# Scan stage of a gated linear recurrence: 32-row key-value products, output in token order

## The reference, cut to what matters

```
def gla_chunk_scan(q, k, v, g, s0):              # L = 32
    b = jnp.cumsum(g, axis=2)
    scores = einsum('nblhk,nbmhk->nbhlm', q * exp(b - b_mid), k * exp(b_mid - b))
    o_intra = einsum('nbhlm,nbmhv->nblhv', where(tri, scores, 0.0), v)
    q_dec, k_dec, decay = q * exp(b), k * exp(b[:, :, -1:] - b), exp(b[:, :, -1])
    def step(s, xs):
        qd, kd, vv, dc = xs
        o = einsum('blhk,bhkv->blhv', qd, s)
        s = dc[..., None] * s + einsum('blhk,blhv->bhkv', kd, vv)
        return s, o
...
    def readout(o, zg):
        on = rms_norm(o, norm_g)                 # over the 128 features of a head
        return (on * silu(zg)) @ w_out
```

## Time and profile before

| | us |
|---|---|
| median of 3 runs | 4289.17 (4285.29 to 4294.36) |
| the profiled execution | 4288.58 |
| its span in the profile | 4286.9 |
| TensorE busy in the span | 4009.6 (94%) |
| VectorE busy | 3233.5 (75%) |
| ScalarE busy | 1963.4 (46%) |

### The profile page before, as it was taken

One profiled execution on the slowest core, in us unless ns is written; L12 is line 12 of the kernel. 1 busy time (PEld: TensorE's weight loads), 2 busy tenths in 40 slices (PEclk: granted clock), 3 DMA queues, 4 the chain that ended last, 5 costly groups with the idle time before them and its releaser, 6 DMA issues. The chain is left out here.

```text
span 4286.9 us, 62093 instructions
## 1 busy us (share of the span) xinstructions
PE 4009.6 (94%) x20354; PEld 3426.2 (80%) x20354; DVE 3233.5 (75%) x5926; ACT 1963.4 (46%) x3726; POOL 1163.7 (27%) x906
## 2 busy tenths in 40 slices
PE   8997988999999899999989999878899999899998
PEld 2886877788888688888867777657899999899997
DVE  2689789998987588888874645558987777577777
ACT  2212235777777522222234434333477778433333
POOL 0322213434333344444422111123122222122221
PEclk9998999999999999999999999889999999999999
DMA  7443126999999899999941111012588888899996
GB/s 285 158 138 128 49 69 228 311 327 350 321 343 338 308 391 373 377 376 374 372 179 50 40 39 39 20 69 69 193 280 273 274 281 296 297 333 331 332 336 225
DMA packets 411882, 1026.06 MB, mean 239 GB/s; under 512 B 33968, under 2 KB 182448, under 8 KB 405680
## 3 DMA queue, kind: packets, MB, share of 16 engines
q1 hardware_dynamic: 296496, 604.22, 39.9%
q0 software_dynamic: 110592, 402.70, 26.2%
q10 hardware_dynamic: 4608, 16.78, 1.1%
HBM read 904.03 MB, written 119.54 MB: 239 GB/s over the span
## 5 line engine op out<-in xcount | busy, mean ns | idle before, releaser
L136 ACT ACTIVATE w_hi<-w_raw 128x1024 fp32r<-128x1024 f32 x536 | 568.3, 1061 | 1152.2 <-PE psum L1425 878.8
L168 PE MATMUL psum<-h_hi,w_hi 128*128 128x512 f32 (+1 forms) x2208 | 877.9, 398 | 90.9 <-PEq L809 30.9
L170 PE MATMUL psum<-h_hi,w_lo 128*128 128x512 f32 (+1 forms) x2208 | 840.8, 381 | 0.0
L169 PE MATMUL psum<-h_lo,w_hi 128*128 128x512 f32 (+1 forms) x2208 | 840.5, 381 | 0.0
L147 DVE TENSOR_TENSOR w_lo<-w_raw,w_hi 128x1024 fp32r<-128x1024 f32 x424 | 519.5, 1225 | 423.5 <-ACT w_hi L136 400.8
L1423 PE MATMUL psum<-a_hie,w_hi 128*128 128x512 f32 (+1 forms) x2048 | 759.1, 371 | 31.0 <-DVE a_loe L1496 31.0
L1425 PE MATMUL psum<-a_hie,w_lo 128*128 128x512 f32 (+1 forms) x2048 | 756.4, 369 | 0.0
L1424 PE MATMUL psum<-a_loe,w_hi 128*128 128x512 f32 (+1 forms) x2048 | 752.1, 367 | 0.0
L1295 POOL DMA_INDIRECT u_rowsg<-in_peer_u_rows,expert_idx x384 | 443.6, 1155 | 1102.8 <-DVE u_rowsg L1052 978.6
L1404 POOL DMA_INDIRECT v_rowse<-in_peer_v,expert_idx x384 | 423.7, 1103 | 825.6 <-DVE row_sume L1505 812.6
L1227 ACT ACTIVATE ojg<-eq_jg,gate_Tg 128x128 fp32r<-128x128 bf16 x1792 | 547.0, 388 | 171.5 <-DVE eq_jg L1075 170.7
(11 more groups left out here) (266 smaller groups left out, 5725.5 us busy)
## 6 DMA issues: line engine op xcount, KB each, us to landing
w_raw<-in_peer_u SPq DMA_DIRECT2D x256, 512.0 KB, 5.9
w_raw<-in_peer_v SPq DMA_DIRECT2D x256, 512.0 KB, 5.7
gates<-stageg SPq DMA_DIRECT2D x28, 2048.0 KB, 16.1
acts<-act_gg SPq DMA_DIRECT2D x128, 256.0 KB, 5.0
gte<-gates SPq DMA_DIRECT2D x32, 1024.0 KB, 8.4
act_fe<-acts SPq DMA_DIRECT2D x128, 256.0 KB, 6.2
ada_w<-in_ada_w SPq DMA_DIRECT2D x12, 2048.0 KB, 8.1
ada_rows<-in_ada_w SPq DMA_DIRECT2D x48, 512.0 KB, 3.9
```

The costliest lines, as they stand in the source:

```text
L136: act.activation(self.weights(s)[0], self.raw[:, slot, :], ACT.Copy).then_inc(self.hi_done, 1)
L168: pe.matmul(out, wh, hi[:, k], start=(k == 0), stop=False)
L169: pe.matmul(out, wh, lo[:, k], start=False, stop=False)
L170: last = pe.matmul(out, wl, hi[:, k], start=False, stop=(k == KC - 1))
```

## The change: what it does, and the diff

Key-value products. A group is now eight matmuls instead of two: for each direction and each chunk r of the block, the 32 rows of that chunk of `kd_tok` and of `v_tok` itself, 128 columns wide, into bank r. `v_by_chunk`, its memset and its four copies per head are gone. All four banks are used by every group, so `kv_free` no longer lets TensorE run one group ahead.

Output. The result now lies in token order, in two halves of 256 tokens in two banks. The masked scores are the stationary side and `v_tok` the moving one; for the states, the 32 columns of `qd` are stationary and the 128-wide state is moving. ScalarE squares each block of 128 x 128 from PSUM and sums along the row in the same instruction; root and reciprocal are 128 x 2. VectorE multiplies from PSUM, TensorE turns the four blocks back (`turn_back`, L1727 in the changed kernel), and VectorE applies gain and gate half by half. The matmul with `ones` and the copy of the output are gone.

Order. On VectorE the next head's decays stand behind the first group and the two scans behind the third and the fourth, and the two query multiplications stand between the two masks. On TensorE the first keys are transposed without product steps ahead of them, two steps now stand behind the second scores, and three steps of tile 4 (two before) stand behind the output.

```
-                            last = pe.matmul(bank(2 * d + x % 2), kd_tok[d][:, g],
-                                             v_by_chunk[:, g].rearrange("p r x -> p (r x)"),
-                                             start=True, stop=True)
+                            for r in range(ROWS):
+                                rows = slice(r * CHUNK, (r + 1) * CHUNK)
+                                last = pe.matmul(bank(r)[:, d * P:(d + 1) * P], kd_tok[d][rows, g], v_tok[rows, g],
+                                                 start=True, stop=True)
...
-                    for d in range(2):
-                        for c in range(XCH):
-                            sl = slice(c * CHUNK, (c + 1) * CHUNK)
-                            last = pe.matmul(bank(3)[:, sl], state[d][:, c], qd[d][:, sl], start=False,
-                                             stop=(d == 1 and c == XCH - 1), skip_group_check=True)
...
+                    for half in range(2):
+                        out = blocks_of(bank(2 + half)[:, 0:2 * P])
+                        for d in range(2):
+                            for g in range(2):
+                                sl = slice((2 * half + g) * P, (2 * half + g + 1) * P)
+                                pe.matmul(out[:, g], probs[d][:, sl], v_tok[:, 2 * half + g],
+                                          start=(d == 0 and g == 0), stop=False, skip_group_check=True)
+                        for d in range(2):
+                            for x in range(2 * ROWS):
+                                c, r = 2 * ROWS * half + x, x % ROWS
+                                last = pe.matmul(out[r * CHUNK:(r + 1) * CHUNK, x // ROWS],
+                                                 qd[d][:, c * CHUNK:(c + 1) * CHUNK], state[d][:, c], start=False,
+                                                 stop=(d == 1 and x == 2 * ROWS - 1), skip_group_check=True)
+                        last.then_inc(S["o_mm"], 1)
...
                     for d in range(2):
-                        if more:
-                            tile(q, u + 1, 2, range(2 * d, 2 * d + 2))
+                        if more and d:
+                            tile(q, u + 1, 2, range(2))
                         to_tokens(h, d + 1)
                         scores(h, d)
+                    if more:
+                        tile(q, u + 1, 2, range(2, 4))
...
-                for x in ("tok_cp", "prob_done", "o_cp"):
+                for x in ("tok_cp", "prob_done", "y_done", "kv_free"):
                     pe.sem_inc(S[x], 1)
-                pe.sem_inc(S["kv_free"], 2)
...
-                            kv = t.psum[:, 4 + 2 * d + x % 2, r * P:(r + 1) * P]
+                            kv = t.psum[:, 4 + r, d * P:(d + 1) * P]
...
                         dve.sem_inc(S["kv_free"], 1)
+                        if more and x == 0:
+                            dve.wait_ge(S["tok_mm"], h * 3 + 3)
+                            decays(h + 1)
+                        elif more and x in (2, 3):
+                            scan(h + 1, x - 2)
```

More of the change, by code:

```diff
@@ L1640, in _ @@
                     m += 1
-                pool.memset(v_by_chunk[:], 0.0).then_inc(S["vc_zero"], 1)
                 def lo(q, j):
@@ L1741, in turn @@
                     if more:
-                        tile(*at, 4, range(KC // 2, KC - 2))
+                        tile(*at, 4, range(KC // 2, KC - 3))
                     output(h)
                     if more:
-                        tile(*at, 4, range(KC - 2, KC))
-                    pe.wait_ge(S["osq"], h + 1)
-                    pe.matmul(bank(2), t.ones[:], osq, start=True, stop=True).then_inc(S["osum"], 1)
-                for x in ("tok_cp", "prob_done", "o_cp"):
+                        tile(*at, 4, range(KC - 3, KC))
+                    turn_back(h)
+                for x in ("tok_cp", "prob_done", "y_done", "kv_free"):
                     pe.sem_inc(S[x], 1)
-                pe.sem_inc(S["kv_free"], 2)
                 for k in range(KC):
@@ L1862, in turn @@
                                           ALU.subtract).then_inc(S["d1"], 1)
-                    dve.wait_ge(S["tok_cp"], h * 3 + 2)
-                    def by_chunk(r0, r1):
-                        for r in range(r0, r1):
-                            rows = slice(r * CHUNK, (r + 1) * CHUNK)
-                            last = dve.tensor_copy(v_by_chunk[rows, :, r], v_tok[rows])
-                        return last
-                    by_chunk(0, ROWS // 2)
                     for d in range(2):
@@ L1888, in turn @@
                                                 S["prob_done"], 1)
+                    masked(0)
                     for d in range(2):
@@ L1891, in turn @@
                         dve.tensor_tensor(qd[d][:], qd[d][:], qs[:], ALU.mult).then_inc(S["qd_done"], 1)
+                    masked(1)
                     dve.wait_ge(S["dc_done"], h * 2 + 2)
-                    if more:
-                        dve.wait_ge(S["tok_mm"], h * 3 + 3)
-                        decays(h + 1)
                     at = 0
@@ L1924, in turn @@
-                    dve.wait_ge(S["y_done"], h + 1)
+                        if more and x == 0:
[3 more added lines that the diff above has]
+                            scan(h + 1, x - 2)
+                    out = [blocks_of(t.psum[:, 6 + half, 0:2 * P]) for half in range(2)]
+                    for half in range(2):
+                        two = slice(2 * half, 2 * half + 2)
+                        dve.wait_ge(S["oroot"], h * 2 + half + 1)
+                        dve.reciprocal(orn[:, two], orn[:, two]).then_inc(S["orstd"], 1)
+                        dve.wait_ge(S["orstd"], h * 2 + half + 1)
+                        dve.tensor_tensor(o[:, two], out[half], orn[:, two].unsqueeze(2).to_broadcast([P, 2, P]),
+                                          ALU.mult).then_inc(S["o_norm"], 1)
@@ new lines, in turn @@
+                    dve.wait_ge(S["z_in"], h + 1)
+                    for half in range(2):
+                        sl = slice(2 * half * P, 2 * (half + 1) * P)
+                        dve.wait_ge(S["o_turned"], h * 2 + half + 1)
+                        dve.scalar_tensor_tensor(out=y[:, bass.ds(h, 1), sl].rearrange("p a n -> p (a n)"),
+                                                 in0=t.psum[:, 4 + half, 0:2 * P], scalar=hs(t.gains[:, 5], h),
+                                                 in1=zs[:, u, sl], op0=ALU.mult, op1=ALU.mult).then_inc(S["y_done"], 1)
@@ L1925, in _ @@
+                    dve.wait_ge(S["y_done"], h * 2 + 3)
                 norm.vector(dve)
                 dve.wait_ge(S["reset_done"], 4)
-                dve.wait_ge(S["vc_zero"], 1)
                 decays(0)
+                for d in range(2):
+                    scan(0, d)
                 turns(dve, turn)
```

67 lines of the change are left out of this document (31 added, 36 removed).

## The result

The changed kernel takes 4194.06 us (median of 4, 4192.4 to 4203.76) against 4291.76 for the kernel before in the same series. The ratio is 0.978, 95% interval 0.977 to 0.980: 2.2% faster. The forecast was 4255 with a range of 4200 to 4285, so the sign was right and the size was not: 34 us were forecast from the profiled execution and about 97 came, which lies outside the range. Span in the profile: 4190.7 us, before 4286.9.

The account below looks back on a forecast made before the run. TensorE's own work, busy 94% of the span, was taken as the bound. The output's 4.8 us a head, seven times, gave 33.6 with the other terms at 0: 4288.6 - 33.6 = 4255 us, range 4200 to 4285.

Parts of the forecast that it names:

- What bounds the kernel, and the clock: TensorE's own work, busy 94% of the span, sets the time; a 128-wide moving side keeps the output at full clock.
- The output, 32 x 0.164: Output products with the states: 0.164 us each, between bounds 0.055 and 0.218; output 7.05 us, a gain of 4.8 per head.
- The key-value products, "I take 0.218": Each 32-row product costs 0.218 us, weight loading the floor; eight per group take 1.74 us as before, so no change.
- The chain of groups, value 0: TensorE and VectorE hand over at each group; TensorE idles about 2.5 us instead of 1.2, covered by what it won.
- the second rival: Key-value and output products both overlap: 4212 us at 0.109 each, 4185 at 0.055; chance 0.30.
- Keys, mask and end of the head, value 0: New 1.0 us key wait offsets the 1.01 us mask wait; the head's end costs 4.3 us, before 4.35.
- Last head, net 0: Gains of 5.6 up to keys, 4.8 output, 4.1 end; losses of 9.5 in groups and 5 by clock.
- the first: Rival: products all serial and sixteen changes of shape per head, 0.17 us each, eat the gain; 4287 or 4277; chance 0.16.
- The third: Rival: GpSimd's splits slow VectorE's decays and scans, 2.2 us per meeting, 4.4 a head; 4296 us, slower; chance 0.12.

Follow-up runs that it names:

- e1: The changed kernel with the 32 output products with the states run strip by strip instead of going round the four strips: 4218.94 us, 0.984 of the kernel before.
- e5: The kernel before with only the output products changed (state as 128-wide moving side, 32 query columns stationary), output not turned back: 4219.30 us, ratio 0.984.
- e2: The changed kernel with each key-value product over all 128 rows of its block, masking of the other chunks left out: 4243.06 us, 0.990 of the kernel before.
- e7: The kernel before with only the 32-row key-value products in one set of banks, VectorE's order and output as before: 4298.46 us, ratio 1.004.
- e3: The changed kernel with VectorE's old order, the next head's decays and both scans ahead of the first state updates: 4225.39 us, 0.986 of the kernel before.
- e10: The changed kernel with the masked-score products of both halves issued ahead of all products with the states: 4186.85 us, 0.978 of the kernel before.
- e13: The changed kernel with moved product steps, split decays with scans last, and both halves' masked scores first: 4181.83 us, 0.976 of the kernel before.
- e14: The changed kernel itself, run again unedited beside three other runs: 4188.26 us, 0.978 of the kernel before.
- e11: The changed kernel with one tile 2 step ahead of each direction's keys and all four last tile 4 steps behind the output: 4185.21 us, ratio 0.977.
- e16: The changed kernel with each group's key-value products ordered in pairs, both directions of a row strip consecutively: 4196.22 us, 0.979 of the kernel before.
- e12: The changed kernel with decays split behind the first and second groups and both scans behind the last: 4181.72 us, 0.976 of the kernel before.
- e15: e13 with one step of tile 4 kept ahead of the output: 4174.72 us, 0.973 of the kernel before.

## Why the prediction was wrong

*What bounds the kernel, and the clock:* right. TensorE's path set the time; the half clock of the output is gone in the seven turns, as argued from L318, and the mean clock of the turn is 1.00.

*The output, 32 x 0.164:* this is the step that failed first. A product costs 0.058, so the output is 4.20 and not 7.05 us, a gain of 7.6 a head and not 4.8. The forecast had the bound 0.055 and kept near the serial row, "a quarter off the row I know"; no row supported that quarter. e1 shows that the strips matter: 0.149 with four neighbours in one strip, 0.063 in turn. In e5 a product costs 0.056 (2407.60 to 2408.50 for sixteen).

*The key-value products, "I take 0.218":* wrong, and the reason with it. The row of a 32-wide moving side showed 0.218 for products one behind the other, which was put down to their weight loads, and I carried it over to 32-row strips as if these could not load side by side. Eight products take 0.65 us with their two changes of shape. e2 uses all rows again, and 5 us a turn come back with it. The Trainium skill, "TensorEngine Tiling (Array Packing)", Key Properties, has different tiles execute weight loads and matmuls in parallel; these runs agree with it, at 0.058 against 0.218.

*The chain of groups, value 0:* the chain's rule was right, its input wrong. With 0.055 the working of the second rival had 4.5 us less from the first group to the output; 4.4 were measured. The handover from VectorE's first update to the next group is 2.26 us (2433.07 to 2435.33), as taken; from a group to the first update it is 0.89 (2432.18 to 2433.07) and not 2.00. e7 and e3 show what the forecast did not price: without VectorE's new order this chain holds TensorE for 3.7 to 6.0 us, and the clock falls behind that.

*Keys, mask and end of the head, value 0:* right. The new wait for the keys is 0.86 us (1.0 worked out) and the first group starts at 17.6 (17.4). From the output to tile 0 it is 3.9 us against 4.35; 4.3 was worked out.

*Last head, net 0:* it gained 10.5 us, and the step that failed is the groups with their clock. They were to lose 9.5 us and the clock 5; from first group to output it is 20.3 us (2691.81 to 2712.11) against 15.5 before (2780.32 to 2795.83), a loss of 4.8, clock included. Group to group is 3.57 us instead of 4.27, and the half clock stretches only short products: a group takes 1.24 instead of 0.73 us in its rows. The other terms held: a gain of 6.2 us up to the first keys (5.6 forecast), of 4.9 in the output up to ScalarE's read of its last part (4.8), and of 4.3 from there to the last y (4.1).

*The rivals.* The second is what happened, at its far end: 4185 worked out, 4194 measured; it had 0.30. Of the first, the changes of shape are there (0.16 us each by e10, 0.17 worked out). If the twelve around the groups cost as much as those in the output, which no run shows, they are 2.6 us a head, too small to eat the gain. The third did not occur: the decay rows between groups are 0.68 us, with no split of GpSimd beside them, and the scan rows 1.76, the second of them with 0.7 us of a split beside it, which had started after it (the rows are in the last section). So it is shown that such meetings did not happen here, not that they would be free. The fall of the clock through standstill, which e3, e7 and e13 show, was in the text only for the last head.

Sum: a turn is 11.9 us shorter in the mean of the seven (12.3 in the one shown; the first and the last, 10.7 and 11.3, are less), which is 83 us. With 10.5 in the last head that is 94 of the 96 us by which the profiled spans differ. The rest lies outside the stage, where two executions of the same changed kernel differ by as much: the stage's first transposes start at 2294.6 us, and at 2289.2 in e14.

## What to carry to other kernels

Where a product uses 32 rows or 32 columns, issue neighbours in different strips and give the wide operand the moving side; price it at a quarter of serial, plus 0.16 us per change of shape, and keep the serial price as the other end. Runs of four in one column strip gave up more than half of that gain. Count TensorE's standstill twice: once for itself, and once for the half clock that can stand behind it. Here it came after a wait of 1.85 us in most turns but not in all, so a change can look worthless while some of its turns gain (e11). Short products make VectorE's chain the bound, so its order has to be changed with them: alone, the one made the kernel slower and the other brought 0.3%.

## What the runs showed that was not expected

- Products in runs of four in one column strip cost 0.149 us, not the 0.218 of the full-width ones (e1), because two strips were still at work at once; pairs in one row strip cost nothing, with four at work (e16). Whether rows against columns plays a part is open.
- A wait of 0.95 us ahead of the output left the clock at 1.00 in all seven turns (e12, e15). Behind one of 1.85 us it fell to 0.50 in four turns of seven (e11) and in six of seven (e13), and took 1.3 us more in the masked-score products of the turn shown. The same wait in the other turns left it at 1.00, so the wait by itself does not decide it; what else does is open.
- GpSimd's split of 1024 columns, begun during a scan on VectorE, left the scan at 1.76 us and took 2.90 itself, where it has 2.40 beside other work. A two-input operation of 768 columns, begun during a split, took 3.16 instead of 0.96. In these rows the one that started first kept its time and the other paid. The rows of GpSimd and VectorE in the changed kernel:

```profile
2440.38 2.90 POOL L147 TENSOR_TENSOR w_lo<-w_raw,w_hi 128x1024 fp32r<-128x1024 f32 x1 [5.09 <-ACT w_hi L136]
...
2455.80 2.93 POOL L147 TENSOR_TENSOR w_lo<-w_raw,w_hi 128x1024 fp32r<-128x1024 f32 x1 [12.52 <-ACT w_hi L136]
```
```profile
2439.33 1.76 DVE L1868 TENSOR_TENSOR_SCAN b<-reset,f 128x768 f32<-128x768 f32 x1 [0.15 <-DVE state L1915]
...
2454.91 0.96 DVE L1876 TENSOR_TENSOR e<-b 128x768 f32<-128x768 f32 x1 [0.19 <-DVE y_heads L1939]
...
2456.39 3.16 DVE L1876 TENSOR_TENSOR e<-b 128x768 f32<-128x768 f32 x1
```
